# A mixing stage reordered, exponentials bound to their logarithms, and the conv relayout in 8 transfers issued by SyncE

## The reference, cut to what matters

```
z = rmsnorm(h) @ w_in                    # columns: A (3 x 384), u 384, v 384, C (2 x 256)
A: y_a = gate_b * conv3(gate_c * xa)                       # short causal depthwise conv
B: y_b = gelu(u) * (W_s[head] @ layernorm(gelu(v)) + b_s)  # within chunks of 128 tokens
C: y_c = silu(layernorm(conv31(c0 * sigmoid(c1)) + bias))  # depthwise, 31 taps
h += concat(rmsnorm(y_a), rmsnorm(y_b), rmsnorm(y_c)) @ w_out
h += (silu(f @ w_gate) * (f @ w_up)) @ w_down ,  f = rmsnorm(h)
h += sigmoid(rmsnorm(h) @ w_ple_gate) * (p @ w_ple_proj)
```

## Time and profile before

| what | us |
|---|---|
| median of the runs | 3324.6 |
| the profiled execution's own time | 3328.0 |
| its span (core 4, the slowest; the others 3306.8 to 3318.1) | 3326.5 |
| TensorE busy | 3107.8 |
| VectorE / ScalarE / GpSimd busy | 2255.8 / 1845.5 / 929.4 |

### The profile page before, as it was taken

How to read it: one execution, slowest core, us unless ns; L and a number is a source line. 1 busy time by engine, 2 the same in 40 slices (tenths; PEclk the granted TensorE clock), 3 DMA queues, 4 the chain that set the end, 5 groups by cost and what they waited for, 6 DMA issues and landing times.

```text
span 3326.5 us, 75661 instructions; the slowest of 8 cores (3306.8 to 3326.5 us)
## 1 busy us (share of the span) xinstructions
PE 3107.8 (93%) x26340; PEld 2512.4 (76%) x26340; DVE 2255.8 (68%) x4932; ACT 1845.5 (55%) x3796; POOL 929.4 (28%) x1308
## 2 busy tenths in 40 slices
PE   7899998999989999899888999989998999989996
PEld 4678876888768877688767888768886788767885
DVE  3688557775477765777558876478765886648855
ACT  4655457544575455754647545475465653656535
POOL 3244122421224222242232322213223231231311
PEclk8899999999999999999999999999999999989998
DMA  8245562445724546255575554625555245643452
GB/s 171 51 77 87 96 107 51 77 80 92 122 40 79 90 82 114 40 89 88 131 133 128 83 86 86 112 40 89 95 92 104 50 79 84 116 78 58 84 90 85
DMA packets 127365, 294.17 MB, mean 88 GB/s; under 512 B 32592, under 2 KB 56272, under 8 KB 126928
## 3 DMA queue, kind: packets, MB, share of 16 engines
q0 software_dynamic: 70656, 244.19, 44.0%
q1 hardware_dynamic: 36608, 37.22, 4.1%
q10 hardware_dynamic: 19728, 7.92, 1.1%
HBM read 508.54 MB, written 12.96 MB: 157 GB/s over the span
## 4 chain that ended last, share of the span: by engine, by line
PE 77%; ACT 5%; DVE 5%; issue 5%; DMA 4%; ACTq 2%; POOL 1%; SPq 0%; DVEq 0%; POOLq 0%
PE PS L812 77%; ACTq L804 2%; DMA WDb<-wD 1%; ACT W L830 1%; ACT SQ L878 1%; ACT L830 1%; DVE NFB L844 1%; DMA GP<-G 1%; DMA XST<-xin 1%; DMA YC<-CO 1%; DVE SQ L844 1%; DVE H L844 0%; DVE TF L844 0%; DVE NF L844 0%; DMA MP<-wsP 0%
## 5 line engine op out<-in xcount | busy, mean ns | idle before, releaser
L812 PE MATMUL PS<-NF,WGh 128*128 128x272 f16 x4224 | 613.8, 279 | 9.5 <-DVE TF L844 4.2
L812 PE MATMUL PS<-NB,WO 128*128 128x272 bf16 x4096 | 498.5, 279 | 22.1 <-ACT W L830 16.9
L812 PEld LDWEIGHTS PS<-NF,WGh 128*128 128x128 f16 x4224 | 409.2, 98 | 96.4 <-issue 21.7
L812 PEld LDWEIGHTS PS<-NB,WO 128*128 128x128 bf16 x4096 | 397.9, 98 | 102.9 <-issue 29.7
L812 PE MATMUL PS<-NFB,WGb 128*128 128x272 bf16 x2816 | 436.9, 279 | 4.1 <-DVE NFB L844 2.5
L844 DVE TENSOR_TENSOR H<-H,PS 128x272 f32<-128x272 f32 (+1 forms) x512 | 258.9, 507 | 261.4 <-PE PS L812 254.0
L837 ACT ACTIVATE TF<-PS 128x272 f32<-128x272 f32 x651 | 257.8, 397 | 272.0 <-PE PS L812 243.9
L844 DVE TENSOR_TENSOR TF<-PS,TF 128x272 f32<-128x272 f32 x704 | 305.2, 437 | 123.9 <-PE PS L812 63.2
L878 ACT ACTIVATE SQ<-H 128x544 bf16<-128x544 f32 x352 | 226.0, 652 | 272.5 <-DVE H L844 261.7
L812 PEld LDWEIGHTS PS<-NFB,WGb 128*128 128x128 bf16 x2816 | 274.8, 98 | 61.2 <-issue 11.2
L812 PE MATMUL PS<-NB,WA 128*128 128x288 bf16 (+1 forms) x2304 | 299.7, 291 | 19.7 <-ACT W L830 9.5
(11 more groups left out here) (159 smaller groups left out, 5607.8 us busy)
## 6 DMA issues: line engine op xcount, KB each, us to landing
WGb<-wGU POOLq DMA_DIRECT2D x176, 512.0 KB, 5.3
WDb<-wD POOLq DMA_DIRECT2D x128, 352.0 KB, 5.5
TZ<-wTZ POOLq DMA_DIRECT2D x32, 640.0 KB, 14.0
WA<-wA POOLq DMA_DIRECT2D x24, 768.0 KB, 11.3
WO<-wO POOLq DMA_DIRECT2D x32, 512.0 KB, 6.6
WO<-wPG POOLq DMA_DIRECT2D x32, 512.0 KB, 6.9
H<-xin SPq DMA_DIRECT2D x16, 544.0 KB, 10.5
WC<-wC POOLq DMA_DIRECT2D x16, 512.0 KB, 9.2
```

The lines of the kernel that those rows point to most:

```text
L812: units.append((lambda e, o, a, b, st=st, sp_=sp_: e.matmul(o, a, b, start=st, stop=sp_, skip_group_check=True), [o], [lh, rh], d))
```

## The change

1. Order of the parts. The new one: c(0), v(0), c(1), relay_in, u(0), rowsums, v(1), conv31, u(1), mixing(0), a(0,0), lnc(0), lnc(1), a(0,1), a(0,2), b_norm(0), yc_norm(0), yc_norm(1), yc_out(0); a(1,0), a_norm(0), mixing(1), a(1,1), a(1,2), b_norm(1), yc_out(1), a_norm(1); w_out.
2. The node of an Exp is bound to the Ln ahead of it: once ScalarE was given the Ln, it is given the Exp next, if that can run.
3. The relay uses 8 transfers instead of 16 each way, all issued by SP, each for both channel halves. The host's layout of TZ and of the conv state follows.
4. Squares of the a, b and yc norms may go to VectorE too (`MSQ`), the copies of `yc_out` to GpSimd too (`YOE`). The scheduler's cost of an issue is 550 ns on SP and 680 on ACT.

```diff
+MSQ = ("act", "dve", "pool")
+YOE = ("act", "dve", "pool")
...
         def choose(e):
             tf = free[e]
+            m = state["chain"]
+            if e == "act" and m is not None and m.npre == 0:
+                q = ready_of(m)
+                if q is not None:
+                    return (max(tf, m.est, q), m, m.lst)
...
+            if e == "act":
+                state["chain"] = n.chain
...
-            d = {"sp": 500.0, "act": 90.0, "pool": 700.0}[eng]
+            d = {"sp": 550.0, "act": 680.0, "pool": 700.0}[eng]
...
-            act(b(both, sub=BB), b(both, sub=BB), AF.Ln, U, scale=inv_n, bias=EPSC[:, 0:1])
+            ln = act(b(both, sub=BB), b(both, sub=BB), AF.Ln, U, scale=inv_n, bias=EPSC[:, 0:1])
             rb = Buf(rbp if half else w2p)
-            act(rb(wide2, sub=BB), b(both, sub=BB), AF.Exp, U, scale=-0.5)
+            ln.chain = act(rb(wide2, sub=BB), b(both, sub=BB), AF.Exp, U, scale=-0.5)
...
-            rb = norm_stats(srcs, inv_n, addlv, stage is not None)
+            rb = norm_stats(srcs, inv_n, addlv, stage is not None, sqe=("act", "pool") if stage is not None else MSQ)
...
                 for p in range(8):
-                    for j in range(2):
-                        dma(GP[p * 16:(p + 1) * 16, j * 8:(j + 1) * 8, 44:180], G[:, j, p, :], 34816,
-                            eng=("sp", "act")[j], small=True)
+                    dma(GP[p * 16:(p + 1) * 16, :, 44:180], G[:, :, p, :], 69632, small=True)
...
-                for j in range(2):
-                    for q in range(8):
-                        dma(YC[:, j, q, :], CO[q * 16:(q + 1) * 16, j * 8:(j + 1) * 8, :], 69632, eng=("sp", "act")[q % 2], small=True)
+                for q in range(8):
+                    dma(YC[:, :, q, :], CO[q * 16:(q + 1) * 16, :, :], 139264, small=True)
...
             c_part(0)
             v_loads()
             v_part(0)
             u_loads()
-            u_part(0)
             c_part(1)
             relay_in()
+            u_part(0)
             a_loads(0)
             rowsums()
             v_part(1)
-            u_part(1)
             a_loads(1)
             conv31()
+            u_part(1)
             a_loads(2)
-            for j in range(3):
-                a_part(0, j)
-                if j == 0:
-                    mixing(0)
-                if j == 1:
-                    lnc_block(0)
-                    lnc_block(1)
+            mixing(0)
+            a_part(0, 0)
+            lnc_block(0)
+            lnc_block(1)
+            a_part(0, 1)
+            a_part(0, 2)
+            b_norm(0)
             yc_norm(0)
             yc_norm(1)
             yc_out(0)
+            a_part(1, 0)
             a_norm(0)
-            b_norm(0)
...
-            for j in range(3):
-                a_part(1, j)
-                if j == 0:
-                    mixing(1)
+            mixing(1)
+            a_part(1, 1)
+            a_part(1, 2)
+            b_norm(1)
             o_loads(0)
             o_loads(1)
...
             yc_out(1)
             a_norm(1)
-            b_norm(1)
```

More of the change, by code:

```diff
@@ L97 @@
     __slots__ = ("id", "opts", "units", "pre", "nxt", "npre", "lst", "bufs", "port", "table", "nbytes",
-                 "eng", "start", "fin", "seq", "est", "peidx", "isdma", "hot", "out", "prio", "val", "vc", "marks", "small", "width", "bank", "tag")
+                 "eng", "start", "fin", "seq", "est", "peidx", "isdma", "hot", "out", "prio", "val", "vc", "marks", "small", "width", "bank", "tag", "chain")
 def dims_of(ap):
@@ L221, in add @@
         n.bank = 0
+        n.chain = None
         n.tag = self.tag
@@ L296, in plan @@
         order = {e: [] for e in ENGS}
-        state = {"port": 0.0, "srv": 0.0, "table": 0, "f32": 1.0}
+        state = {"port": 0.0, "srv": 0.0, "table": 0, "chain": None}
         pedone = [False] * self.npe
@@ L1177, in lnc_block @@
                 stt(vb(wide2, sub=BB), bq(both, sub=BB), 1.0 / 256, vb(wide2, sub=BB), ALU.mult, ALU.subtract, U, port=False)
-                act(vb(wide, sub=(0, 1)), vb(wide, sub=(0, 1)), AF.Ln, U, bias=EPSC[:, 0:1])
-                act(vb(wide, sub=(0, 1)), vb(wide, sub=(0, 1)), AF.Exp, U, scale=-0.5)
+                ln = act(vb(wide, sub=(0, 1)), vb(wide, sub=(0, 1)), AF.Ln, U, bias=EPSC[:, 0:1])
+                ln.chain = act(vb(wide, sub=(0, 1)), vb(wide, sub=(0, 1)), AF.Exp, U, scale=-0.5)
                 for j in range(2):
@@ L1292, in a_norm @@
                 normed(srcs, [vcol(l, 24, j) for j in range(3)], [NBT[u][:, j, :] for j in range(3)], 1.0 / 384, addlv=1)
[L1294 to L1297, removed]
-            u_part(0)
-            c_part(1)
-            relay_in()
-            a_loads(0)
-            rowsums()
-            v_part(1)
-            u_part(1)
-            a_loads(1)
-            conv31()
-            a_loads(2)
-            for j in range(3):
-                a_part(0, j)
-                if j == 0:
-                    mixing(0)
-                if j == 1:
-                    lnc_block(0)
-                    lnc_block(1)
-            yc_norm(0)
-            yc_norm(1)
-            yc_out(0)
-            a_norm(0)
-            b_norm(0)
             ow = []
@@ L1325, in o_loads @@
                 ow.append(t)
-            for j in range(3):
-                a_part(1, j)
-                if j == 0:
-                    mixing(1)
+            c_part(0)
+            v_loads()
+            v_part(0)
+            u_loads()
+            c_part(1)
+            relay_in()
+            u_part(0)
+            a_loads(0)
+            rowsums()
+            v_part(1)
+            a_loads(1)
+            conv31()
+            u_part(1)
+            a_loads(2)
+            mixing(0)
[5 more added lines that the diff above has]
+            b_norm(0)
+            yc_norm(0)
+            yc_norm(1)
+            yc_out(0)
+            a_part(1, 0)
+            a_norm(0)
+            mixing(1)
+            a_part(1, 1)
+            a_part(1, 2)
+            b_norm(1)
             o_loads(0)
```

10 lines of the change are left out of this document (5 added, 5 removed).

## The result

The changed kernel takes 3287.9 us (median of four runs, 3281.0 to 3291.2) against 3324.6: a ratio of 0.9887, with a 95% interval of 0.9858 to 0.9915. That is 37 us less, where 57 were forecast. The time lies 21 us above the forecast of 3267 and inside the range.

The account below looks back on a forecast made before the run. TensorE, busy 93%, was taken as the bound, with 116.6 us idle in the mixing stages. 18 - 9 + 53 - 5 = 57 us off the profiled 3328.0 gives 3271, 3267 as median; range 3225 to 3305.

Parts of the forecast that it names:

- the cover of YC: Between conv31 and lnc_block(0): about 11 us of matmuls cover YC's landing at +9 to +11; costed at nothing.
- The signs listed in the prediction: No ACT-queue relay rows, conv31 waiting 1 to 4 us for GP, no norm bunch, third mixing stage 100 to 102 us.
- GP's arrival: Ahead of conv31: shorter cover 20 us, lone queue 8, against 19 lost before; net 9 us worse, bounds 19 better, 35 worse.
- ScalarE's issues: Relay issues leave ScalarE: 18 gained of 19.6 us lost after conv31; 8.8 lost behind GP issues counted under GP's arrival.
- Norms spread: Four norms bunched behind a_part(0)'s last block lose 73 us; spreading gains 53, 20 stay in norm chains; bounds 26 and 73.
- Second C block ahead of u: After V in the mixing stage: the scheduler already runs it ahead of the WU matmuls, so it gains nothing.
- Exp bound to Ln: Norms on ScalarE: an op freeing PSUM stands behind Exp; 5 us worse, bounds 10 worse and 8 better.
- lists and costs: Squares and YC copies allowed on VectorE and GpSimd, issues costed 550 and 680: nothing, between 8 worse and 8 better.
- (a): In the mixing stages, the scheduler keeps a norm bunch; norms gain 26, time 3295; chance 0.23 together with (d).
- (b): In the mixing stages, u's blocks fill the GP wait and norm chains hide: 107 us gained, 3218; chance 0.19.
- (c): conv31 waits for GP behind too short a cover, from 10.6 us per pass on; slower, 3338; chance 0.08.
- (d): The reorder of parts does nothing since the scheduler sorts by due times; only ScalarE's issues matter, 3298; 0.23 with (a).

Follow-up runs that it names:

- The experiment with one A block more: The changed kernel with lnc_block(0) and lnc_block(1) moved behind a_part(0, 1), as before the change: 3331 to 3338 us, ratio 1.0030.
- the hold: Loads of WO wait until all YC transfers land; here with new relay and order, without binding and lists, against the kernel before: 3248.2 and 3253.5 us.
- the hold kernel: The changed kernel with the loads of WO made dependent on the YC transfers having landed: median 3221.6 us, ratio 0.9695.

## Why the prediction was right or wrong

**The step that failed** is the cover of YC: "I cost it at nothing; each microsecond by which that cover fails costs eight." It cost some 65 us (3287.9 against 3221.6), more than the whole distance to the forecast. The sentence had the rule right and the size wrong, twice. First, YC was put at +9 to +11 behind conv31, "if they queue as before"; it lands at +17 in the third pass, because WO's loads are in flight at the same time. In the third pass of before, two are issued at 894.33, ahead of the YC transfers of the earlier trace rows, and a third only at 907.05, when YC had landed (8.9 us behind conv31); here the second and third go out at 894.5 and 897.0, in YC's flight. With the loads held the last of it has landed by +10.7 there, which is the value of the prediction. Second, the 11 us of cover were matmuls counted as if nothing else stood between. There were as many (11.4 us, until 899.7). But the XA op that TensorE needs next shares an in-order engine with the squares of YC, and waits behind these. The experiment with one A block more shows this: more cover in matmuls, and 46 us slower.

Here are DMA queues of the changed kernel (packets, MB, share of 16 engines), YC's transfers from 895 to 897, and the same from 898 to 904:

```profile
q1 hardware_dynamic: 1100, 0.57, 99.5%
...
q0 software_dynamic: 268, 0.97, 81.4%
q1 hardware_dynamic: 616, 0.33, 20.6%
```

With hardly any weights beside it, SP's queue passes 1100 packets in 2 us, 550 in a microsecond. Beside weights it passes 616 in 6 us, 103 in a microsecond, while the weights hold the engines for 81% of the time. The price of YC is the company that it has.

The signs listed in the prediction didn't catch this. All four came: no ACT rows, waits for GP of 1.8 to 3.2 us behind the first pass, no bunch, and a third mixing stage of 102.65 us. And the forecast didn't fail first in the norm chains or in GP's arrival, as it said.

**ScalarE's issues: 18 forecast, 37 by themselves.** The prediction took 18 of the 19.6 and let the 8.8 behind the GP issues be void, since TensorE would only come to conv31 sooner. The relay alone won both, 7.9 more as faster matmuls, and some of it in the first pass, to which the prediction gave nothing. In the new order it is the other way round: with ScalarE's 16 issues back, the kernel is no slower than with all on SP (3268 and 3271). The gain of a step depends on the order that it stands in. How much of the 37 comes from the changed costs of issue was not tried.

**GP's arrival: 9 worse forecast.** 28 us of waiting for GP were expected and 25.2 came, by two errors of opposite sign. The arrival was put 1 us later for the single queue, and it isn't later: in the seven passes from the second the GP copy ends 14.9 to 18.0 us behind the second C block before and 15.5 to 16.9 after (in the third +17.2, and +16.2: 864.3 and 880.5). And the scheduler put one block of u_part(1) ahead of conv31, not three, as the third pass shows:

```profile
877.17 1.10 PE L822 MATMUL PS<-NB,WU 128*128 128x272 bf16 x8
...
880.77 5.44 PE L822 MATMUL PS<-GP,TZ 128*128 128x168 bf16 x50 [2.50 <-ACT GP L847]
```

On the single queue: GP's packets once the weights are through, in the changed kernel from 876 to 878 and in the kernel before from 882 to 884.

```profile
q1 hardware_dynamic: 1259, 0.32, 140.2%
...
q1 hardware_dynamic: 649, 0.17, 76.5%
q10 hardware_dynamic: 643, 0.16, 69.3%
```

One queue passes 1259 in 2 us and two together 1292, at like shares of the engines' time. So here the engines are the limit, not the queue. The 42 ns a packet and the 132% from which the prediction derived a slower lone queue were no evidence: a lone queue's packet times add up to 140% as well, since they overlap among themselves. The Trainium skill, "DMA: Bandwidth & Descriptors", section "Rules for kernel authors", says that spreading over issuing engines saves only issue time; the trace agrees (1259 against 1292). The same page's "Queues, rings and completion order" has an engine take turns between its queues by packet. Beside the weights the profile counts 616 to 268 here (and 176 to 148 between SP and ACT in the earlier trace rows); whether its packets are those of the page no run here shows, so this is no test of equal turns.

**Norms spread: 53 forecast, rightly placed.** The bunch is gone. Windows of the changed kernel where the yc norms are:

```profile
920.10:929.30 9.20, 8.12 (x72) 5.67 (x71) 8.10 (x17) 8.90 (x16) 1.25 (x4) 1.00 0.03 5
```

A stretch as long as that of the earlier trace rows has 72 matmuls instead of 13, at a clock of 1.00 instead of 0.68. 1.1 us of it are idle, where 2.5 a pass were allowed for. The order alone cuts the mixing stages by 53.8 us, of which it gives back 14 in the gate and up products. That giving back was not in the prediction, which called the other stages hardly touched.

**Second C block ahead of u: nothing.** Right: the 64 WC matmuls stand where they stood, behind V and ahead of WU.

**Exp bound to Ln: 5 us worse; lists and costs: nothing.** Alone, the binding is 15 us worse (bounds were 10 worse and 8 better), so outside. With the lists, in the new order, it is some 22 us better. The mechanism named (what frees PSUM stands behind Exp) fits the longer waits for copies and squares of the one run, but why the sign turns is open.

**The sum.** By pieces: 37 for the relay and 36 for the order make 3252 (3251 measured, with the hold). Binding and lists bring 29 more then (3222), and YC's lateness takes 66: 3288. That the time fell inside the range is luck: a relay, and binding and lists, sized too small, against a cover that failed. **The rivals:** (a) the bunch isn't kept. (b) All of it comes, 3218: its parts exist, and the hold kernel is at 3222, but not as the change stands. (c) conv31 waits at most 7.1 us for GP; the mechanism of (c), a relay behind too short a cover, is real, but at YC, where the prediction gave it half of 8%. (d) The reorder is none: refuted by the order alone, which is worth 36 us.

**Open:** the ple stages are 7 us longer in the changed kernel (372.3 against 364.9, to the last matmul). The loss sits in two of them, the one between the two halves (58.1 to 66.0) and the last (54.4 to 58.0); the six others are 4 us shorter in the sum. The binding alone lengthens the same two, by half as much (61.4 and 56.5), and wins it back in the six others (363.7 in all). Which of binding and lists gives the 22 us is open as well.

## What to carry to other kernels

When a transfer is moved, write down what else is on the DMA queues in its new flight time; its landing as seen before holds only in the same company, and a bulk load that isn't urgent can be made to wait for it. Count as cover only matmuls whose feeding ops don't stand behind the late transfer on an in-order engine. Two gains that were measured one by one add up only as long as neither uses the other's slack; here 37 and 36 gave 37, and a dependency on four loads a pass gave the rest back.

## What the runs showed of the hardware

One queue of small SBUF transfers (about 255 bytes a packet) passed 1259 packets in 2 us, two queues 1292, at 140% and 146% of the 16 engines' time: shares over 100% don't need two queues. With packets of about 520 bytes one queue passed 1100 in 2 us; beside weight loads it fell to about a fifth (616 in 6 us). A stop of TensorE of 4.1 us in 6.8 was followed by a granted clock of 0.75 for the next 5.8 us, although TensorE was busy throughout; of the 65 us that late YC data cost, 21 were such slower matmuls.
